# A gated-delta-rule heads loop: output gate read from PSUM, causal mask added by TensorE, modulation product moved

## The reference, cut to what matters

```
g = cumsum(g)                                              # per chunk
decay = exp(where(lower, g[t] - g[s], -inf))               # causal mask inside the exponent
L = where(strict, (k * beta) @ k.T * decay, 0)
T = inverse of (I + L)                                     # triangular
u, w = T @ (v * beta), T @ (k * beta * exp(g))
attn = (q @ k.T) * decay
o = state part + attn @ v_new
o = rmsnorm(o, norm_w) * silu(z)                           # the output gate
mod = cond @ ada_w[1] + ada_b[1]                           # shift, scale (8 column tiles) of the next layer
```

## Time and profile before

| | |
|---|---|
| median of 3 runs | 1618.76 us |
| profiled execution, own time | 1621.4 us |
| its span | 1619.6 us |
| TensorE busy | 1554.8 us, 96% |
| VectorE busy | 1109.9 us, 69% |
| ScalarE busy | 932.7 us, 58% |
| GpSimd busy | 493.4 us, 30% |
| heads loop, from the first level_d(0) to finish step 0 of round 7 | 197.20 to 327.95 us |

### The profile page before, as it was taken

How to read it: one execution, slowest core, us unless ns; L and a number is a source line. 1 busy time by engine, 2 the same in 40 slices (tenths; PEclk the granted TensorE clock), 3 DMA queues, 4 the chain that set the end, 5 groups by cost and what they waited for, 6 DMA issues and landing times.

```text
span 1619.6 us, 37025 instructions
## 1 busy us (share of the span) xinstructions
PE 1554.8 (96%) x13269; PEld 1429.3 (88%) x13269; DVE 1109.9 (69%) x2304; ACT 932.7 (58%) x1763; POOL 493.4 (30%) x405
## 2 busy tenths in 40 slices
PE   7899999899999999999999999999999999999998
PEld 6899877798998899888999999999999888888886
DVE  3787768656556653776478888798888555555554
ACT  1766567744555555545354444799898544555554
POOL 4000278661000040000067777766565100000000
PEclk9999979899999999999999999999999999999999
DMA  9668412454443344247455555544444666666663
GB/s 295 219 184 278 150 55 82 133 163 130 151 131 118 111 156 131 79 157 156 104 150 167 168 168 172 162 143 135 140 131 143 182 194 194 193 192 190 194 193 127
DMA packets 211832, 255.89 MB, mean 158 GB/s; under 512 B 15912, under 2 KB 193804, under 8 KB 211724
## 3 DMA queue, kind: packets, MB, share of 16 engines
q1 hardware_dynamic: 211723, 254.39, 53.2%
HBM read 253.29 MB, written 1.05 MB: 157 GB/s over the span
## 4 chain that ended last, share of the span: by engine, by line
PE 72%; DVE 11%; issue 5%; DMA 4%; ACT 4%; SPq 2%; DVEq 0%; ACTq 0%
PE ps L2253 22%; PE ps L2861 22%; PE ps L2843 10%; PE ps L2831 3%; DMA raw<-in_u_experts 3%; PE ps L2273 2%; PE ps L2551 2%; DVE raw L2014 2%; SPq L580 2%; PE ps L2628 1%; DVE w_lo L1396 1%; PE ps L2451 1%; DMA arena<-in_ada_w 1%; DVE arena L2067 1%; PE ps L2648 1%
## 5 line engine op out<-in xcount | busy, mean ns | idle before, releaser
L742 POOL TENSOR_TENSOR w_lo<-raw,w_hi 128x1024 fp32r<-128x1024 f32 x128 | 307.6, 2406 | 337.7 <-ACT w_hi L1265 337.6
L2253 PE MATMUL ps<-x_hi,w_hi 128*128 128x256 f32 x1088 | 315.3, 290 | 8.3 <-DVE w_lo L1396 3.0
L2253 PE MATMUL ps<-x_hi,w_lo 128*128 128x256 f32 x1088 | 308.2, 283 | 0.0
L2253 PE MATMUL ps<-x_lo,w_hi 128*128 128x256 f32 x1088 | 308.2, 283 | 0.0
L2212 DVE TENSOR_TENSOR w_lo<-raw,w_hi 128x1024 fp32r<-128x1024 f32 x124 | 152.0, 1226 | 143.2 <-ACT w_hi L1374 143.2
L1374 ACT ACTIVATE w_hi<-raw 128x1024 fp32r<-128x1024 f32 x124 | 131.6, 1061 | 168.0 <-PE ps L2861 168.0
L2253 PEld LDWEIGHTS ps<-x_hi,w_hi 128*128 128x128 f32 x1088 | 209.1, 192 | 15.3 <-issue 6.0
L2253 PEld LDWEIGHTS ps<-x_lo,w_hi 128*128 128x128 f32 x1088 | 209.2, 192 | 1.3 <-issue 1.2
L2253 PEld LDWEIGHTS ps<-x_hi,w_lo 128*128 128x128 f32 x1088 | 209.0, 192 | 0.0
L1265 ACT ACTIVATE w_hi<-raw 128x1024 fp32r<-128x1024 f32 x128 | 134.9, 1054 | 113.4 <-DVE raw L2014 113.2
L2806 PE MATMUL ps<-x_hi,w_hi 128*128 128x256 f32 x576 | 166.3, 289 | 10.6 <-ACT arena L1287 9.7
(11 more groups left out here) (446 smaller groups left out, 3563.7 us busy)
## 6 DMA issues: line engine op xcount, KB each, us to landing
raw<-in_u_experts SPq DMA_DIRECT2D x512, 128.0 KB, 2.7
raw<-in_v_experts SPq DMA_DIRECT2D x128, 512.0 KB, 4.3
arena<-in_ada_w SPq DMA_DIRECT2D x18, 1024.0 KB, 7.8
raw<-in_a_w_in SPq DMA_DIRECT2D x12, 1024.0 KB, 5.7
arena<-in_a_w_in SPq DMA_DIRECT2D x12, 1024.0 KB, 5.7
raw<-in_b_w_in SPq DMA_DIRECT2D x8, 1024.0 KB, 5.7
arena<-in_b_w_in SPq DMA_DIRECT2D x8, 1024.0 KB, 5.6
raw<-in_w_in SPq DMA_DIRECT2D x8, 1024.0 KB, 5.6
```

The source lines that it names most:

```text
L742: pool.tensor_tensor(UTL[e], UT[e % 2], UTH[e].bitcast(F32), ALU.subtract).then_inc(utl_ready, 1)
L2253: ins = mm(o[:, b * S:b * S + S], w[:, slot, kk, b * P:b * P + P], xx[:, (kk + turn) % KC, :], start=(kk == 0 and n == 0), stop=(kk == k - ...
```

## The change

On TensorE: a new step `setup_masks(n)` adds the mask to ROWS in PSUM, by an identity product with `negu`, now bf16, for each of four 128-column blocks; it stands between finish step 3 and level_p(3). `setup_values` waits for the exponentials (h_dt). `modulator` sums two slices instead of one (four products), and is that of round f, ahead of level_p(4); in round 0 there is none, and that of round 7 stands in the finish behind the loop. `setup_keys` goes behind level_d(1), finish step 2 behind level_p(2), the norm sums ahead of level_p(5). Finish step 3 counts h_og differently, step 5 waits for the gate too. `level_p` and `level_d` can begin with `spare` products of 128x512 bf16 (`keep_wide`) into the bank that they write next: two ahead of level_d(0) and one ahead of level_d(4) in every round; further ones stand in round 0 (levels 1, 3, 5) and round 7 (levels 2, 4) where f or n is absent. In level_d(0) the wait for the round before's last close stands ahead of the spares.

On VectorE: `decays` is gone; `betas` stands ahead of close_level(2), `lowers` ahead of close_level(3), mask_level(1) ahead of `normalised_k`. `gated` multiplies A2, read from PSUM, by the norm weight and ZB, after mask_level(4) and `modulator(f)`; `normed` is one product by RNo.

On ScalarE: the exponentials read ROWS in PSUM; the copy of A2 to OS is gone; the copies of v (`setup_v`) go ahead of the spreads.

On GpSimd: the last of the seven additions of a modulation tile is gone. In round 7 split_x_half(1, 0) and (1, 1) on VectorE take the places of `betas` and `lowers`.

```diff
@@ gpsimd
-                for half, done in ((4, 8), (2, 12), (1, 14)):
+                for half, done in ((4, 8), (2, 12)):
                     pool.wait_ge(mod_sum, 15 * i + (24 + done))
                     for kk in range(half):
-                        pool.tensor_tensor(w[:, kk, :], w[:, kk, :], w[:, kk + half, :], ALU.add).then_inc(mod_sum, 1)
+                        pool.tensor_tensor(w[:, kk, :], w[:, kk, :], w[:, kk + half, :], ALU.add).then_inc(mod_sum, half if half == 2 and kk else 1)
@@ scalar
             def setup_decays(r):
+                if r.at:
+                    act.wait_ge(h_kd, r.count(2))
+                    act.wait_ge(h_at, r.count(2))
+                    act.wait_ge(h_lt, r.count(2))
                 for g in range(2):
                     act.wait_ge(h_dta, r.nth(g))
                     for cc in range(2):
-                        act.activation(two(DT[g])[:, cc, :], two(DT[g])[:, cc, :], ACT.Exp,
+                        act.activation(two(DT[g])[:, cc, :], ROWS[g][:, cc * 128:cc * 128 + 128], ACT.Exp,
                                        bias=NGT[:, cc, r.heads[g]:r.heads[g] + 1]).then_inc(h_dt, 1)
-            def finish_out(r):
+            def finish_squares(r):
+                for g in range(2):
+                    act.wait_ge(h_o, r.nth(g))
+                    act.activation(SQo[g], A2[g], ACT.Square).then_inc(h_sq, 1)
+
+            def finish_norms(r):
                 if r.at:
                     act.wait_ge(h_out, r.count(2, 2))
-                for g in range(2):
-                    act.wait_ge(h_o, r.nth(g))
-                    act.activation(OS[g], A2[g], ACT.Copy).then_inc(h_os, 1)
-                    act.activation(SQo[g], A2[g], ACT.Square).then_inc(h_sq, 1)
-
-            def finish_norms(r):
@@ scalar, inner
                 if f:
-                    finish_out(f)
+                    finish_squares(f)
+                if n:
+                    setup_v(n)
                 spread(i, 0)
                 spread(i, 1)
-                if n:
-                    setup_v(n)
                 spread(i, 2)
@@ vector
-            def normed(r, g):
+            def gated(r):
                 if r.at >= 6:
                     v.wait_ge(z_late, 1)
+                for g in range(2):
+                    v.wait_ge(h_sq, r.nth(g))
+                    zb = ZB[:, r.heads[g], :]
+                    v.scalar_tensor_tensor(zb, A2[g], COLS[:, CAN:CAN + 1], zb, ALU.mult, ALU.mult).then_inc(h_os, 1)
+
+            def normed(r, g):
                 v.wait_ge(h_orn, r.nth(g))
                 v.wait_ge(h_os, r.nth(g))
-                v.scalar_tensor_tensor(OS[g], OS[g], COLS[:, CAN:CAN + 1], RNo[g], ALU.mult, ALU.mult).then_inc(h_og, 1)
-                v.wait_ge(h_og, r.nth(g, 1, 1, 2))
                 zb = ZB[:, r.heads[g], :]
-                v.tensor_tensor(zb, OS[g], zb, ALU.mult).then_inc(h_out, 1)
+                v.tensor_tensor(zb, zb, RNo[g], ALU.mult).then_inc(h_out, 1)
@@ vector, inner
                 if n:
-                    decays(n)
+                    betas(n)
                 else:
                     split_x_half(1, 0, ZB[:, 0:8, :])
+                close_level(i, 2)
                 mask_level(i, 3)
-                if n:
-                    betas(n)
-                close_level(i, 3)
-                mask_level(i, 4)
                 if n:
                     lowers(n)
                 else:
                     split_x_half(1, 1, ZB[:, 0:8, :])
+                close_level(i, 3)
+                mask_level(i, 4)
+                if f:
+                    modulator(f)
+                    gated(f)
                 close_level(i, 4)
                 if n:
                     v.wait_ge(h_spread, i.count(6, 6))
                     starts(n)
                 mask_level(i, 5)
-                modulator(i)
@@ tensor
+            def setup_masks(r):
                 for g in range(2):
                     pe.wait_ge(h_eg, r.nth(g))
                     pe.wait_ge(h_xm, r.nth(g))
+                    for cc in range(2):
+                        ins = mm(ROWS[g][:, cc * 128:cc * 128 + 128], ident16, negu, start=False, stop=True, skip_group_check=True)
+                    ins.then_inc(h_dta, 1)
+
+            def setup_values(r):
+                for g in range(2):
+                    pe.wait_ge(h_dt, r.nth(g, 2))
@@ tensor, modulator
                 for cc in range(2):
-                    ins = mm(MODP[:, cc:cc + 1], RAW[MOD_SLOT[r.side]][:, 0, cc * 128:cc * 128 + 128], ones[:, 0:1], start=True, stop=True)
+                    for half in range(2):
+                        ins = mm(MODP[:, cc:cc + 1], RAW[MOD_SLOT[r.side]][:, half, cc * 128:cc * 128 + 128], ones[:, 0:1],
+                                 start=(half == 0), stop=(half == 1))
                 ins.then_inc(raw_free, 1)
+            def keep_wide(bank_, n):
+                for _ in range(n):
+                    mm(bank_[:, :], ident16, BG3, start=True, stop=True)
@@ tensor, inner
                 level_p(i, 0)
-                level_d(i, 0)
+                level_d(i, 0, 2)
                 if f:
                     finish(f, 0)
-                level_p(i, 1)
+                level_p(i, 1, 0 if f else 2)
                 if f:
                     finish(f, 1)
+                level_d(i, 1, 0 if f else 2)
                 if n:
                     setup_keys(n)
-                level_d(i, 1)
+                level_p(i, 2, 0 if n else 1)
                 if f:
                     finish(f, 2)
-                level_p(i, 2)
                 if n:
                     setup_rows(n)
-                level_d(i, 2)
+                level_d(i, 2, 0 if n else 1)
                 if f:
                     finish(f, 3)
+                if n:
+                    setup_masks(n)
                 level_p(i, 3)
                 if f:
                     finish(f, 4)
-                level_d(i, 3)
+                level_d(i, 3, 0 if f else 2)
                 if n:
                     setup_values(n)
-                level_p(i, 4)
-                level_d(i, 4)
+                if f:
+                    modulator(f)
+                level_p(i, 4, 0 if n else 2)
+                level_d(i, 4, 1)
                 if f:
                     finish(f, 5)
                 if n:
                     setup_low(n)
-                level_p(i, 5)
-                modulator(i)
                 if i.at + 2 < GQ:
                     norm_sums(Round(i.at + 2))
+                level_p(i, 5, 0 if f else 2)
                 level_d(i, 5)
```

40 lines of the change are left out of this document (21 added, 19 removed).

## The result

The kernel after took **1631.38 us**, the median of 5 runs (1629.56 to 1636.97), beside 1618.76 of the kernel before: ratio **1.0084**, 95% interval 1.0061 to 1.0107. That is +12.6 us. The forecast was 1625.5 with a range up to 1631.0, so the measured time lies 0.4 us above the upper end; the sign was right, the size was half (6.7 forecast). The rival "the clock falls in round 0 all the same" (chance 0.13) had 1631.7.

What follows compares the result with a forecast made beforehand. TensorE was taken to fill the first half of a round's chain, VectorE the second. Terms 1.7 - 3.1 - 0.8 + 6.8 + 1.0 + 1.2 - 0.1 = +6.7 us took the median from 1618.76 to 1625.5, range 1613 to 1631.

Steps and rivals of the forecast that it cites:

- the clock falls in round 0 all the same: Rival: spares fail in round 0; round 0 +0.3, round 1 +2.0, total +12.9, 1631.7 us; chance 0.13.
- The steady round: A round with norm sums goes from 15.28 to 17.0 us, +1.7; rounds 2 to 5 together +6.8.
- both halves: Level_d(0) to level_p(4) goes from 9.4 to 10.65 us; from there to the next level_d(0), 5.9 to 6.35.
- the masks: Setup_masks on TensorE in the first half of a round: 0.3 us, bounds 0 and 0.58.
- the modulator: Four products between setup_values and level_p(4): 0.9 us in the first half, bounds 0.3 and 0.9.
- the two gated products: On VectorE in the second half: 0.48 us each, taken as the upper value, 0.96 for both.
- VectorE's chain sets the round: Rival, level_p(4) to level_d(0): TensorE absorbs the additions, a round is 14.5, total -9.2, 1609.6 us; chance 0.13.
- half absorbed: Rival: the round becomes TensorE's bare work, 15.7 us; total -1.0, 1617.8 us; chance 0.18.
- round 7 keeps its clock: Rival: spares let half of the stretch 312 to 322 go at double speed, -3.5; total +3.2, 1622.0 us; chance 0.13.
- cost nothing: The modulator's old place lay in the second half, where TensorE had room, so it added no time there.
- I take it that they hold the full clock: Spares in rounds 0 and 1 keep the full clock: round 0 13.7 us (-3.1), round 1 17.0 (-0.8).
- +1.2 with the clock as before: Round 7: modulator +0.9, spares at half clock +0.6, one normed product -0.3, if the clock falls and returns as before.

Runs made afterwards that it cites:

- moved, two: Kernel before with the modulator moved ahead of level_p(4) of the next round, still two products, seventh GpSimd addition kept: 1623.64 us, ratio 1.0005.
- moved, four: Kernel before with the modulator moved ahead of level_p(4) of the next round and made four one-column products, six GpSimd additions: 1636.25 us, ratio 1.0100.
- experiment 7: Kernel before with modulator moved, doubled or both; kernel after without spares, with modulator back or moving 64 columns: 1623.64 to 1641.79 us.
- experiment 4: Kernel after with the modulator back at its old place and size (two products, seven GpSimd additions): 1626.22 us, ratio 1.0036.
- experiment 2: Kernel after without any spare products, everything else kept: 1648.63 us, ratio 1.0186.
- experiment 1: Kernel after run once more with no edit: 1636.55 us, ratio 1.0078 to the kernel before.
- experiment 5: Kernel after with the norm sums behind level_p(5) again: with spares 1633.32 us, ratio 1.0064; without spares 1643.45 us, ratio 1.0133.

## Why the prediction was wrong, by its steps

**Right.** The steady round: 17.04 for 17.0, both halves to 0.05 us, with hole, spares and price of the gate where they were put; round 6 16.37 for 16.3; GpSimd off the path. That came from taking each half of the chain with the engine that is full in it. Within it terms were off both ways and cancelled: the masks 0.42 in the chain for 0.3, the modulator 0.79 for 0.9, the two gated products 0.86 for 0.96, and the keys' wait, which the sum did not have. So the mechanism is shown, and the agreement to 0.05 us is partly luck. The estimate of 0.39 for one gated product from the Trainium skill ("VectorE: DVE Perf Modes", § The TRN2 errata) is below the 0.474 of the record, as it was for the half width; but it is what lies between the starts of two back to back (0.86 less 0.474). The sum took the record for both, which is too dear by 0.1 for the pair. The Trainium skill's sentence on weight loads pulled ahead of matmuls in flight ("TensorE: Matmul & The Clock Gate", opening table) does not hide the modulator's here: the eight stand in the chain with 0.79. The rivals "VectorE's chain sets the round" and "half absorbed" fell with the windows of 17.04, "round 7 keeps its clock" with its 0.52. One sentence was half wrong: that the modulator "cost nothing" in its old place. In "moved, two" and "moved, four" of experiment 7 the second half is 0.43 shorter by the chain when it goes (5.86 for 6.29). That is not TensorE's: VectorE's copy of 0.16 leaves the chain there, and the second normed product takes 0.42 instead of 0.72, for a reason that no row shows. The sum did not rest on it, since the new second half was added up anew.

**The step that failed: "I take it that they hold the full clock"**, and with it -3.1 and -0.8 for rounds 0 and 1. The spares of the change didn't hold it in round 0 of the two profiled executions (17.00 and 17.22 at 0.80, where the same instructions at 1.00, experiment 4, take 14.70, itself 1.0 above the 13.7 of the sum), nor in round 1 in one of them. The low stretch became shorter, two of about 7 us for one of 17 (and one of 27 without spares, experiment 2), but it was not gone: rounds 0 and 1 took 36.8 us, and 34.4 in experiment 1, where the sum has 30.7 (34.7 before). Windows of 2 us around the first level_d(0), for after (it begins at 200.06) and for experiment 4 (at 198.39), whose TensorE instructions are the same up to there:

```profile
198.00:200.00 2.00, 1.00 (x65) 0.67 (x58) 1.83 (x6) 1.07 (x4) 2.00 (x5) 1.00 0.00 0
200.00:202.00 2.00, 1.86 (x67) 1.10 (x68) 0.61 (x3) 0.00 (x0) 2.00 (x4) 0.66 0.04 8
```

```profile
196.00:198.00 2.00, 0.98 (x65) 0.83 (x66) 1.82 (x7) 1.41 (x6) 2.00 (x4) 1.00 0.01 4
198.00:200.00 2.00, 2.00 (x70) 0.91 (x68) 1.00 (x5) 0.00 (x0) 2.00 (x5) 1.00 0.03 8
```

In after the clock falls just behind the first level_d(0), after 4 us in which TensorE was busy half the time. In experiment 4 the same thin stretch stands ahead of the loop (0.98 of 2 us), the same spares follow it, and the clock never fell in that round. So the spares around level_d(0) cannot be relied on to prevent the fall, and whether they come too late for it these rows do not decide.

**The second error is one of kind**: the clock was treated as one event of round 0 (a rival with 0.13) and otherwise "as before". It falls in steady rounds too, in places that differ between executions: in the kernel before once the modulator is moved and doubled, and in the changed order without spares even with the modulator back (0.80, 0.83 and 0.82 in rounds 1, 2 and 5). And round 7, "+1.2 with the clock as before", took 5.2 more, with 27 us at the lower level (323.5 to 351; before, 13.5, from 309 to 322.4, of which the prediction's 312 to 322 is only a part). Replacing the two rounds' gains by what was measured, 17.00 for 13.7 and 19.84 for 17.0, adds 6.1 to the sum's +6.7: +12.8, and the medians are 12.6 apart. That agreement is partly luck: the profiled execution is the slowest of the five (1637.0, clock 0.983; median 0.989), and it closes only with more terms: 12.8, +1.6 for round 4, -1.3 for the queue's stall of round 3 that is gone, +4.0 for round 7, +2.2 behind the loop, +1.2 at its start and -4.7 given back later are +15.8, where 15.6 were measured.

**What stays open.** That the kernel before loses its clock only with moving and doubling together is shown (1.0005, 1.0019, 1.0100); that few columns are part of it is suggested (two intervals that overlap a little). Why the exchange of keys and finish step 2 lowers the clock, and why the same instructions lose it near 199 (experiment 5), near 201 (after, experiment 1) or not at all in round 0 (experiment 4), no run here tells. No run put spares into the thin 4 us ahead of the first level_d(0), which would test whether that is what matters.

## What to carry to other kernels

Where the windows by stage show TensorE between its two clock levels, price an edit twice: by its work on the chain, and by what it does to the clock in the rounds around it; here four one-column products of 0.9 us cost 3 us of work and about 10 by the clock. Do not book a gain from a clock that spares are to hold before a run shows it: in this sum it was 3.9 us, and the profiled execution had none of it. Put spare products only where the clock column is low and the engine waits anyway; in rounds at 1.00 that are bound by TensorE they cost 0.57 a round in the kernel before and 0.31 in the kernel after, and they have to be tried in the final order, since what held one order lost 20 us more than expected in another. Before taking load from one engine, ask which waits come next in the same half of the chain: here 0.6 us of relief for VectorE brought 0.16.

## What the runs showed of the hardware that was not expected

- The granted clock is not a property of the program: of nine executions of one kernel on one chip eight had means of 0.981 to 0.993 and times from 1627.5 to 1643.4 us, some 1.2 us for each thousandth of the mean clock; the ninth had 0.937 at 1641.7. A profile shows one of these, so kernels are better compared by the median clock over their executions than by the dips of one profile.
- Two edits with little or no effect on the clock alone (0.985 beside 0.986, and 0.988 beside 0.987) give 0.978 together.
- Four one-column 128x128 fp32 products stand in the timeline with 0.95 us, and with 1.00 when 64 columns are moved: with so few columns the time hardly depends on how many they are.
- Two scalar_tensor_tensor instructions of 128x256 from PSUM have records of 0.474 us each (0.480 from SBUF), and together occupy 0.86: the second begins 0.39 after the first.
